# Cached index keys of a decode step: the query columns become the stationary operand in four column tiles, and the weighted sum over heads becomes two matrix products

## The chip, the cores and the metric

The kernel runs on one core of one Trainium2 chip. The metric is the device time of one execution in microseconds (us). All data are float32.

## The reference, cut to what matters

One layer is computed for 1024 prompt tokens and for 8 sample sequences of one new token each: a feed-forward half step, a mixer (sparse attention beside a gated recurrence), a second feed-forward half step. The change lies in the mixer, in the *indexer* of the sample sequences. Every sample sequence has 8192 cached index keys of 64 numbers, in 64 pages of 128 keys. Each key gets one score from eight index heads, and the 256 best keys are attended.

```python
def indexer_scores(qi, wi, kidx, valid):
    logits = jnp.einsum('bqhd,bld->bqhl', qi, kidx) * (HEAD_DIM_IDX ** -0.5)
    score = jnp.einsum('bqh,bqhl->bql', wi * (N_HEADS_IDX ** -0.5), jax.nn.relu(logits))
    return jnp.where(valid, score, -jnp.inf)
...
ki_past = cache_kidx[page_table].reshape(B, past, HEAD_DIM_IDX)
score = indexer_scores(qi, wi, ki_all, valid[None])
_, idx = lax.top_k(score, n_sel)
```

## The kernel before, in words

Five engines run programs of their own and meet at semaphores. The work follows an order written out by hand in each engine's program; nothing plans it at run time. TensorE computes the mixer's input projection in *units* (`unit`): one unit is 8 matrix products of 128 rows of contraction, each with 344 moving columns (L723) or 256 (L728). A float32 product leaves two records in the trace, so a unit leaves 16.

The part that the change touches is a loop of 32 rounds (`ROUNDS`), about 915 to 1125 us after the start of the span. In each round, one eighth of the pages of two sequences is scored, and beside it runs one step of a 32-step bitwise search for the threshold of the prompt's top 256 (`NBITS`). Round r on each engine:

- GpSimd gathers 128 rows of 1024 numbers (16 keys each) by an indirect DMA into one of four buffers `KX` (L614). Partitions 0 to 63 belong to one sequence, 64 to 127 to the other.
- TensorE turns the block by eight 128x128 transposes (L781, `turn_keys`), so that a pair of keys lies on the 128 partitions; it runs one unit; then `key_logits` (L790) makes eight products with 128 key columns stationary and 32 moving query columns `QB` (two parities of key, eight heads, two sequences). The result is 128 partitions by 256 numbers in PSUM bank 5 or 6.
- ScalarE copies the turned keys out of PSUM (`keys_out`, L1143), sums three compare results for the search (`pass_counts`, three L1149), and copies the unit's result (L1115).
- VectorE compares three score blocks for ScalarE (L1367) and counts three more itself (L1370). Then comes `reduce_keys` of the round before: two fused maximum-and-multiply operations on 64 partitions (L1322) and one reduction over the eight heads (L1326) into the score table `SDEC`. Then it waits for ScalarE's sums and does four small operations (L1376, L1353, L1354, L1355) that set the next candidate of the search.

Waits that couple the engines: transposes of round r wait until ScalarE has copied the keys of r-1; `key_logits` of r waits for the copied keys of r and for the reduction of r-2; ScalarE's sums come behind its copy of the keys, in its program order; the next search step on VectorE waits for ScalarE's sums.

Before the loop, GpSimd sends the sample queries through a scratch tensor to `QB` (L626, L630) and the head weights to `WDEC` (L633, L637), then issues output DMAs and four masks (L660). VectorE scales `WDEC` (L1346). After the loop TensorE waits for the last keys to be reduced and for VectorE's preparation of the recurrence (L1483 to L1490) before the level products (L856).

Of the kernel before, what the change touches and what calls it, by code (L numbers as in the profile page):

```python
# [9 lines left out]
def build_decoder_step(nc, I, O):  # L10
# [8 lines left out]
    ALU, ACT, AX = mybir.AluOpType, mybir.ActivationFunctionType, mybir.AxisListType  # L19

    P = 128
# [23 lines left out]
    with ctx:  # L45
# [319 lines left out]
        KXT = BIG[:, 3 * C4 + 2560:3 * C4 + 4608].rearrange("p (u c) -> p u c", c=1024)  # L365
        DPROD = BIG[:, 3 * C4 + 2048:3 * C4 + 2304].rearrange("p (u c) -> p u c", c=P)
        RELU = BIG[:, 3 * C4:3 * C4 + 2048].rearrange("p (u c) -> p u c", c=1024)
# [3 lines left out]
        def score(b):  # L371
# [8 lines left out]
        KIW = AUX[:, 0:9 * 72].rearrange("p (b c) -> p b c", c=72)  # L380
        WIS = AUX[:, 648:648 + 72].rearrange("p (b h) -> p b h", h=H)
        JUNK = BIG[:, o_kv + 2304:o_kv + 2560].bitcast(mybir.dt.uint8)
        DCMP = K3[:, 2, 9 * HD:9 * HD + 258].bitcast(mybir.dt.bfloat16).rearrange("p (g k) -> p g k", k=PAGE + 1)
# [35 lines left out]

        WDEC = SMALL[:, 0:32].rearrange("p (g h) -> p g h", h=H)  # L420
        DCNT, GTC, PCC = SMALL[:, 32:36], SMALL[:, 36:40], SMALL[:, 40:48]
# [13 lines left out]
        qi_s, q_s = dram("scratch_qi", [512, NB]), dram("scratch_q", [512, NB])  # L435
        w_s, sn_s = dram("scratch_w", [NB, H]), dram("scratch_new_score", [NB, 1])
        hid_s = dram("scratch_hidden", [P, FT * TOK]).rearrange("p (f t) -> p f t", t=TOK)
# [8 lines left out]
        qid_turned, sn_ready = sem("qid_turned"), sem("sn_ready")  # L446
        scratch_out, qb_zero, qb_in, w_in_dec, sn_in = (sem(x) for x in (
            "scratch_out", "qb_zeroed", "qb_in", "wdec_in", "sn_in"))
        sdec_filled = sem("sdec_filled")
# [156 lines left out]
        def pool_mixer(pool, G, link):  # L606
# [14 lines left out]
            G.memset(SDECF, NEG).then_inc(sdec_filled, 1)  # L621
            G.memset(QB[:, :, :, :], 0.0).then_inc(qb_zero, 1)
            nc_ok = nc.allow_non_contiguous_dma(reason="eight sample columns")
            with nc_ok:
                pool.wait_ge(unit_out, N1)
                pool.dma_start(qi_s.rearrange("(t p) b -> p t b", p=P), QIT[:, :, SEQ:TOK]).then_inc(scratch_out, 16)  # L626
                pool.wait_ge(scratch_out, 16)
                pool.wait_ge(qb_zero, 1)
                for par in range(2):
                    pool.dma_start(QB[64 * par:64 * par + 64, par, :, :],  # L630
                                   qi_s.rearrange("(h d) b -> d h b", d=HD)).then_inc(qb_in, 16)
                pool.wait_ge(wis_ready, 1)
                pool.dma_start(w_s, WIS[0:NB, 8, :]).then_inc(scratch_out, 16)  # L633
                pool.wait_ge(scratch_out, 32)
                for half in range(2):
                    src = w_s.rearrange("(g u) h -> u g h", u=2)[half:half + 1].to_broadcast([64, 4, H])
                    pool.dma_start(WDEC[64 * half:64 * half + 64, :, :], src).then_inc(w_in_dec, 16)  # L637

# [11 lines left out]
                pool.dma_start(sn_s, SN).then_inc(scratch_out, 16)  # L650
                pool.wait_ge(scratch_out, 48)
                pool.wait_ge(sdec_filled, 1)
# [50 lines left out]
        def pe_mixer(pe, cols, mean, var):  # L703
# [80 lines left out]
            def key_logits(r):  # L784
                gp = r // 8
                pe.wait_ge(kxt_a, r + 1)
                if r >= 2:
                    pe.wait_ge(dix_read, 2 * r - 2)
                for j in range(8):
                    last = M(PS[:, 5 + r % 2, 32 * j:32 * j + 32], KXT[:, r % 2, P * j:P * j + P],  # L790
                             QB[:, :, :, 2 * gp:2 * gp + 2], start=True, stop=True)
                last.then_inc(dix_done, 1)
            pe.wait_ge(qb_in, 32)
            for r in range(ROUNDS):
                turn_keys(r)
                unit(N1 + WOVEN + r)
                key_logits(r)
            pe.wait_ge(kxt_a, ROUNDS)
            pe.wait_ge(dix_read, 2 * ROUNDS)

# [283 lines left out]
        def act_mixer(act, A, link, square, sd, gain):  # L1084
# [54 lines left out]
            def keys_out(r):  # L1139
# [15 lines left out]

            def block_copy(t, lv):
# [116 lines left out]
        def dve_mixer(dve, V, link, step, centre, sqsum, scale):  # L1273
# [39 lines left out]

            def reduce_keys(r):
                gp, sub = divmod(r, 8)
                dve.wait_ge(dix_done, r + 1)
                if r >= 2:
                    dve.wait_ge(dix_red, r - 1)
                for half in range(2):
                    rows = slice(64 * half, 64 * half + 64)  # L1320
                    ps = PS[rows, 5 + r % 2, 0:256].rearrange("p (k h s) -> p k h s", h=H, s=2)[:, :, :, half]
                    V.scalar_tensor_tensor(DPROD[rows, r % 2, :].rearrange("p (k h) -> p k h", h=H), ps, 0.0,  # L1322
                                           WDEC[rows, gp:gp + 1, :].to_broadcast([64, 16, H]),
                                           ALU.max, ALU.mult).then_inc(dix_read, 1)
                dve.wait_ge(dix_read, 2 * r + 2)
                V.tensor_reduce(SDEC[:, gp, 16 * sub:16 * sub + 16],  # L1326
                                DPROD[:, r % 2, :].rearrange("p (k h) -> p k h", h=H), AX.X, ALU.add).then_inc(dix_red, 1)
            for i in range(6 * H):
# [33 lines left out]
            for i in range(NBITS):  # L1362
# [10 lines left out]
                if i:  # L1373
                    reduce_keys(i - 1)
# [3 lines left out]
            reduce_keys(NBITS - 1)  # L1378

            def sample_compare(k):  # L1380
                if k == 0:
                    dve.wait_ge(sn_in, 32)
                    dve.wait_ge(dix_red, ROUNDS)
# [1541 lines left out]
```

## Time and profile before

| | us |
|---|---|
| median of 3 runs | 2485.77 (2480.25 to 2489.41) |
| time of the profiled execution | 2480.91 |
| span of its trace | 2478.8 |
| TensorE matmul busy | 2392.3 (97%) |
| VectorE busy | 1684.4 (68%) |
| ScalarE busy | 698.6 (28%) |
| GpSimd busy | 861.4 (35%) |
| mean granted TensorE clock | 0.98 of full speed |

The 2.1 us between the span and the execution's time lie around the program. A busy share is an average over stages; the stage of the 32 rounds has to be read by itself. Matmul records overlap, so the pace of a run of matmuls is read from its starts, or from its piece in the chain of waits, not from the length of one record.

### The profile page before, as it was taken

How to read it: one execution, taken by the hardware profiler on the slowest of the kernel's cores; microseconds unless marked ns; L12 is line 12 of the kernel's file. 1: busy time of each engine (PE TensorE's matmuls, PEld its weight loads, DVE VectorE, ACT ScalarE, POOL GpSimd, SP SyncE). 2: the span in 40 equal slices, each digit the busy share in tenths (PEclk: the TensorE clock that was granted, in tenths of full speed). 3: DMA queues.
4: the chain of work that ended last, by engine and by line, in shares of the span. 5: the costliest groups of instructions: out<-in, count | busy, mean ns of one | idle time of the engine just before them, and what ended most of it. 6: DMA issues, size and time to landing. Idle time of an engine off the chain costs nothing.

```text
span 2478.8 us, 33700 instructions
## 1 busy us (share of the span) xinstructions
PE 2392.3 (97%) x12445; PEld 1986.0 (80%) x12445; DVE 1684.4 (68%) x2737; ACT 698.6 (28%) x1399; POOL 861.4 (35%) x916
## 2 busy tenths in 40 slices
PE   8999999999999999999998899999999999999996
PEld 7888888888886547887777777788888888888885
DVE  6666666588963287898777855435675665677886
ACT  2122222200033166662222245512322222210014
POOL 5344444445563111110000022413344444445570
PEclk9999999999999999999998889999999999999998
DMA  6021213374201213330000021112012222157301
GB/s 179 18 94 52 90 64 103 111 278 161 81 22 34 69 52 98 94 86 18 2 18 1 11 62 38 48 35 68 9 60 85 69 72 74 60 190 266 141 18 69
DMA packets 136928, 192.34 MB, mean 78 GB/s; under 512 B 18472, under 2 KB 85144, under 8 KB 136512
## 3 DMA queue, kind: packets, MB, share of 16 engines
q1 hardware_dynamic: 129328, 169.71, 20.5%
q0 software_dynamic: 7440, 20.49, 3.1%
q8 instruction: 102, 1.67, 0.3%
q14 instruction: 58, 0.48, 0.1%
HBM read 160.12 MB, written 30.06 MB: 77 GB/s over the span
## 4 chain that ended last, share of the span: by engine, by line
PE 86%; DVE 9%; issue 2%; ACT 2%; POOL 1%; DMA 1%; SPq 0%; DVEq 0%; POOLq 0%; ACTq 0%
PE ps L1955 37%; PE ps L2049 15%; PE ps L723 8%; PE ps L728 6%; PE ps L1068 4%; PE ps L956 2%; PE ps L790 2%; PE ps L930 2%; PE ps L2052 2%; PE ps L768 1%; PE ps L846 1%; PE ps L943 1%; PE ps L781 1%; ACT big L1135 1%; DVE big L1384 0%
## 5 line engine op out<-in xcount | busy, mean ns | idle before, releaser
L1955 PE MATMUL ps<-big 128*128 128x258 f32 x1760 | 410.5, 381 | 5.1 <-DVE big L2368 4.6
L1955 PEld LDWEIGHTS ps<-big 128*128 128x128 f32 x1760 | 333.0, 190 | 57.1 <-issue 7.7
L2220 ACT ACTIVATE down_weights<-ps 128x258 f32<-128x258 f32 x370 | 142.8, 387 | 700.4 <-PE ps L1955 700.3
L2488 DVE TENSOR_TENSOR down_weights<-ps,down_weights 128x258 f32<-128x258 f32 x330 | 139.4, 425 | 261.6 <-ACT down_weights L2220 186.9
L723 PE MATMUL ps<-acts,weight_ring 128*128 128x344 f32 x768 | 236.7, 458 | 0.0
L723 PEld LDWEIGHTS ps<-acts,weight_ring 128*128 128x128 f32 x768 | 141.8, 190 | 77.3 <-issue 12.4
L2049 PE MATMUL ps<-big,aux 128*128 128x258 f32 x840 | 193.1, 385 | 4.0 <-DVE big L2601 4.0
L2796 POOL TENSOR_TENSOR big<-weight_ring 128x256 f32<-128x256 f32 x100 | 75.3, 755 | 334.8 <-PE ps L1955 300.1
L2049 PEld LDWEIGHTS ps<-big,aux 128*128 128x128 f32 x840 | 160.8, 192 | 30.1 <-DVE big L2601 5.7
L728 PE MATMUL ps<-weight_ring,acts 128*128 128x256 f32 (+3 forms) x720 | 176.6, 401 | 0.0
L728 PEld LDWEIGHTS ps<-weight_ring,acts 128*128 128x128 f32 (+1 forms) x720 | 129.1, 184 | 34.1 <-issue 3.1
L2049 PE MATMUL ps<-big,weight_ring 128*128 128x258 f32 x600 | 137.5, 381 | 0.6 <-DVE weight_ring L2647 0.5
L1955 PE MATMUL ps<-big,aux 128*128 128x258 f32 x512 | 131.6, 381 | 0.9 <-DVE down_weights L2488 0.9
L2049 PEld LDWEIGHTS ps<-big,weight_ring 128*128 128x128 f32 x600 | 113.4, 190 | 19.2 <-issue 2.0
L1955 PE MATMUL ps<-big,weight_ring 128*128 128x258 f32 x480 | 120.8, 381 | 0.0
L1955 PE MATMUL ps<-acts,weight_ring 128*128 128x258 f32 x480 | 114.6, 382 | 4.0 <-DVE acts L1703 1.8
L1955 PE MATMUL ps<-weight_ring,big 128*128 128x258 f32 x464 | 118.1, 381 | 0.0
L1068 PE MATMUL ps<-big,weight_ring 128*128 128x258 f32 x512 | 113.4, 382 | 0.8 <-ACT big L1203 0.8
L1955 PEld LDWEIGHTS ps<-big,aux 128*128 128x128 f32 x512 | 96.9, 190 | 16.1 <-DVE down_weights L2488 1.7
L1068 PEld LDWEIGHTS ps<-big,weight_ring 128*128 128x128 f32 x512 | 96.9, 190 | 15.1 <-ACT big L1203 1.0
L1955 PEld LDWEIGHTS ps<-acts,weight_ring 128*128 128x128 f32 x480 | 90.7, 190 | 18.5 <-DVE acts L1703 2.2
L1955 PEld LDWEIGHTS ps<-big,weight_ring 128*128 128x128 f32 x480 | 91.1, 190 | 13.4
(443 smaller groups left out, 4605.8 us busy)
## 6 DMA issues: line engine op xcount, KB each, us to landing
big<-scratch_hidden SPq DMA_DIRECT2D x12, 2838.0 KB, 11.1
weight_ring<-ffn_wd SPq DMA_DIRECT2D x8, 2816.0 KB, 9.8
scratch_hidden<-down_weights SPq DMA_DIRECT2D x40, 516.0 KB, 2.8
weight_ring<-ffn_wg SPq DMA_DIRECT2D x20, 1024.0 KB, 7.9
weight_ring<-ffn_wu SPq DMA_DIRECT2D x20, 1024.0 KB
down_weights<-ffn_wd SPq DMA_DIRECT2D x4, 2816.0 KB, 20.7
weight_ring<-w_in SPq DMA_DIRECT2D x9, 1024.0 KB, 5.3
big<-x_prompt SPq DMA_DIRECT2D x8, 512.0 KB, 5.6
```

The source lines that it names most:

```text
L723: last = M(PS[:, unit_bank(u), 0:TW], w[:, k, P * a:P * a + P], ACTS[:, k, cols(x)], start=k == 0, stop=k == DT - 1)
L728: last = M(PS[0:rows, unit_bank(u), 0:a], ACTS[:, k, P * x:P * x + rows], w[:, k, :], start=k == 0, stop=k == DT - 1)
L790: last = M(PS[:, 5 + r % 2, 32 * j:32 * j + 32], KXT[:, r % 2, P * j:P * j + P], QB[:, :, :, 2 * gp:2 * gp + 2], start=True, stop=True)
L930: last = M(PS[:, k0, 0:min(512, n - c)], QT[rows, h // 2, P * b:P * b + P], K3[rows, h // 4, c:min(c + 512, n)], start=True, stop=True)
L956: last = M(PS[:, 2 + bi % 2, HD * h:HD * h + HD], probs_turned(i)[:, P * j:P * j + P], KV[:, j, c:c + HD], start=j == 0, stop=j == b)
L1068: last = M(PS[:, Y_BANK[y], 0:TQ], w[:, k, P * (d % 2):P * (d % 2) + P], src, start=k == 0, stop=k == DT - 1)
L1955: last = M(PS[:, 3 * e + bank, 0:TQ], lhs[:, i, :], rhs[:, i, :], start=begin and i == 0, stop=end and i == n - 1, skip_group_check=True)
L2049: last = M(PS[:, 3 * e + bank, 0:TQ], lhs[:, i, P * e:P * e + P], rhs[:, i, :], start=begin and i == 0, stop=end and i == 4 and rest is No ...
L2052: last = M(PS[:, 3 * e + bank, 0:TQ], rest[0][:, P * e:P * e + P], rest[1], start=False, stop=end, skip_group_check=True)
L2220: A(st(e, c), PS[:, 3 * e, 0:TQ], ACT.Copy).then_inc(cp_done, 1)
L2488: V.tensor_tensor(out, PS[:, 3 * e + bank, 0:TQ], st(e, part), ALU.add).then_inc(add_done, 1)
L2796: G.tensor_tensor(part(e, 2), operand(e, 0, 0), operand(e, 1, 0), ALU.subtract).then_inc(su_done, 1)
```

## The change

`key_logits` swaps its operands: the 32 query columns (rearranged by GpSimd into `QG`) are stationary, in four column tiles of 32 (PSUM partitions 0-31, 32-63, 64-95, 96-127), and each tile has 256 of the 1024 key columns moving. The head now lies on the partitions, so the weighted sum over heads is a contraction: VectorE only takes the maximum with zero (`relu_keys`, one operation on 128x256 from PSUM to `KREL`), and TensorE makes two products (`key_scores`) with 128 columns of `KREL` stationary and 16 columns of a small table `WSEL` moving, into PSUM bank 7. These come two rounds later, between the transposes and the unit. Every eight rounds ScalarE copies a finished table from bank 7 into `SDEC` (`page_scores`, two copies of 64x128). The table `WSEL` is built once by VectorE from the identity and the head weights, which GpSimd brings by two DMAs out and eight DMAs in.

```diff
@@ GpSimd, before the loop
-                pool.dma_start(w_s, WIS[0:NB, 8, :]).then_inc(scratch_out, 16)
-                pool.wait_ge(scratch_out, 32)
-                for half in range(2):
-                    src = w_s.rearrange("(g u) h -> u g h", u=2)[half:half + 1].to_broadcast([64, 4, H])
-                    pool.dma_start(WDEC[64 * half:64 * half + 64, :, :], src).then_inc(w_in_dec, 16)
+                for u in range(2):
+                    pool.dma_start(w_s[:, :, u], WIS[u:NB:2, 8, :]).then_inc(scratch_out, 16)
+                pool.wait_ge(scratch_out, 48)
+                pool.wait_ge(qb_in, 32)
+                G.tensor_copy(QG.rearrange("p g (x u) -> p g x u", u=2),
+                              QB.rearrange("p r h (g u) -> p g (r h) u", u=2)).then_inc(consts, 1)
+                for x in range(8):
+                    pool.dma_start(WROW[16 * x:16 * x + 16, :], w_s.rearrange("g h u -> (h u) g")).then_inc(w_in_dec, 16)
@@ TensorE
                 if r >= 2:
-                    pe.wait_ge(dix_read, 2 * r - 2)
-                for j in range(8):
-                    last = M(PS[:, 5 + r % 2, 32 * j:32 * j + 32], KXT[:, r % 2, P * j:P * j + P],
-                             QB[:, :, :, 2 * gp:2 * gp + 2], start=True, stop=True)
+                    pe.wait_ge(dix_read, r - 1)
+                for c in range(4):
+                    rows = slice(32 * c, 32 * c + 32)
+                    last = M(PS[rows, 5 + r % 2, 0:2 * P].rearrange("p (u x) -> p u x", u=2),
+                             QG[:, gp, :],
+                             KXT[:, r % 2, :].rearrange("p (u c x) -> p u c x", u=2, c=4)[:, :, c, :], start=True, stop=True)
                 last.then_inc(dix_done, 1)
+            def key_scores(r):
+                gp, sub = divmod(r, 8)
+                pe.wait_ge(dix_read, r + 1)
+                if gp and sub == 0:
+                    pe.wait_ge(dix_red, 2 * gp)
+                for j in range(2):
+                    at = 16 * sub + 8 * j
+                    last = M(PS[:, 7, 0:2 * P].rearrange("p (b c) -> p b c", b=2)[:, :, at:at + 8],
+                             KREL[:, r % 2, P * j:P * j + P], WSEL[:, gp, :, :], start=True, stop=True)
+                last.then_inc(dix_scored, 1)
             for r in range(ROUNDS):
                 turn_keys(r)
+                if r >= 2:
+                    key_scores(r - 2)
                 unit(N1 + WOVEN + r)
                 key_logits(r)
+            key_scores(ROUNDS - 2)
+            key_scores(ROUNDS - 1)
             pe.wait_ge(kxt_a, ROUNDS)
-            pe.wait_ge(dix_read, 2 * ROUNDS)
+            pe.wait_ge(dix_red, 8)
@@ ScalarE
+            def page_scores(gp):
+                act.wait_ge(dix_scored, 8 * gp + 8)
+                if gp == 0:
+                    act.wait_ge(sdec_filled, 1)
+                for half in range(2):
+                    rows = slice(64 * half, 64 * half + 64)
+                    A(SDEC[rows, gp, 0:PAGE], PS[rows, 7, P * half:P * half + PAGE], ACT.Copy).then_inc(dix_red, 1)
             for r in range(ROUNDS):
                 keys_out(r)
+                if r >= 9 and r % 8 == 1:
+                    page_scores(r // 8 - 1)
                 pass_counts(r)
                 unit(N1 + WOVEN + r)
+            page_scores(3)
@@ VectorE
-            def reduce_keys(r):
-                gp, sub = divmod(r, 8)
+            def relu_keys(r):
                 dve.wait_ge(dix_done, r + 1)
                 if r >= 2:
-                    dve.wait_ge(dix_red, r - 1)
-                for half in range(2):
...
-                    V.scalar_tensor_tensor(DPROD[rows, r % 2, :].rearrange("p (k h) -> p k h", h=H), ps, 0.0,
...
-                dve.wait_ge(dix_read, 2 * r + 2)
-                V.tensor_reduce(SDEC[:, gp, 16 * sub:16 * sub + 16],
...
+                    dve.wait_ge(dix_scored, r - 1)
+                V.tensor_scalar(KREL[:, r % 2, :], PS[:, 5 + r % 2, 0:2 * P], 0.0, None, ALU.max).then_inc(dix_read, 1)
-            dve.wait_ge(w_in_dec, 32)
-            dve.wait_ge(sdec_filled, 1)
-            link(V.tensor_scalar(WDEC, WDEC, KSCALE, None, ALU.mult))
+            dve.wait_ge(w_in_dec, 128)
+            link(V.tensor_reduce(PICK.rearrange("p (x b) -> p x b", b=2),
+                                 IDENT.rearrange("p (x h b) -> p x b h", h=H, b=2), AX.X, ALU.add))
+            for gp in range(4):
+                link(V.tensor_scalar(WSEL[:, gp, :, :].rearrange("p b x -> p x b"), PICK.rearrange("p (x b) -> p x b", b=2),
+                                     WROW[:, gp:gp + 1], KSCALE, ALU.mult, ALU.mult))
```

## Rows read from the trace of the kernel before

**Rows 1.** Page, part 1: busy us, share of the span, instructions.

```profile
PE 2392.3 (97%) x12445; PEld 1986.0 (80%) x12445; DVE 1684.4 (68%) x2737; ACT 698.6 (28%) x1399; POOL 861.4 (35%) x916
```

**Rows 2.** Chain that ended last, rounds 12 to 15 and its end: start us, us, what.

```profile
1000.70 4.63 PE ps L723 x16
1005.33 1.71 PE ps L790 x16
1007.03 0.91 PE ps L781 x8
1007.94 4.63 PE ps L723 x16
...
1021.25 3.46 PE ps L728 x16
1024.70 1.71 PE ps L790 x16
1026.40 0.91 PE ps L781 x8
1027.31 3.46 PE ps L728 x16
...
1100.18 1.78 DVE big L1367 x3
1106.02 1.88 DVE big L1367 x3
1111.95 1.88 DVE big L1367 x3
1117.89 2.65 DVE big L1367 x3
```

**Rows 3.** Timeline of one late round: start us, us, engine, line [idle before <-releaser].

```profile
1110.17 0.61 DVE L1322 SCALAR_TENSOR_TENSOR big<-ps,small 64x128 f32<-64x128 f32 x2
1110.82 0.28 DVE L1326 TENSOR_REDUCE down_weights<-big 128x16 f32<-128x128 f32 x1
1111.02 0.16 DVE L1376 TENSOR_SCALAR rejected<-counts 128x6 int32<-128x6 f32 x1
```

**Rows 4.** Timeline of an earlier round, transposes to the next search step.

```profile
1081.13 1.07 PE L781 MATMUL ps<-ident,weight_ring 128*128 128x128 f32 x8
1082.24 1.02 ACT L1143 ACTIVATE big<-ps 128x1024 f32<-128x1024 f32 x1 [1.98 <-PE ps L781]
1085.96 0.37 ACT L1115 ACTIVATE big<-ps 128x256 f32<-128x256 f32 x1
1086.08 0.17 DVE L1376 TENSOR_SCALAR rejected<-counts 128x6 int32<-128x6 f32 x1
1087.02 1.88 DVE L1367 TENSOR_SCALAR big<-down_weights,candidate 128x1024 f32<-128x1024 f32 x3
```

**Rows 5.** Timeline of products on parts of the array: row halves (L768), column halves (L901).

```profile
908.72 1.99 PE L768 MATMUL ps<-big 64*128 64x512 f32 x8 [0.33 <-ACT big L1135]
910.63 0.85 PE L723 MATMUL ps<-acts,weight_ring 128*128 128x344 f32 x2
1200.13 1.15 PE L901 MATMUL ps<-big 128*64 128x64 f32 x32
```

**Rows 6.** Chain that ended last, the same products: whole array (L896), column halves (L901).

```profile
1196.44 3.75 PE ps L896 x32
1200.20 1.11 PE ps L901 x32
```

**Rows 7.** Groups of VectorE, by form: plain copies out of PSUM, mean ns of one.

```profile
L2329 DVE COPY acts<-ps 128x512 f32<-128x512 f32 x10 | 6.4, 686 | 8.0 <-PE ps L1930 8.0
L1286 DVE COPY big<-ps 128x384 f32<-128x384 f32 x8 | 4.4, 553 | 41.4 <-PE ps L739 41.4
```

**Rows 8.** Timeline of GpSimd and VectorE before the loop.

```profile
862.62 1.28 POOL L637 DMA_DIRECT2D small<-scratch_w  x2 [3.94 <-DMA scratch_w<-aux]
...
914.52 0.18 DVE L1346 TENSOR_SCALAR small<-small 128x32 f32<-128x32 f32 x1
914.92 0.29 POOL L660 TENSOR_SCALAR_AFFINE_SELECT down_weights<-down_weights 128x128 f32<-128x128 f32 x1 [12.66 <-DVE down_weights L1340]
915.31 2.09 DVE L1367 TENSOR_SCALAR big<-down_weights,candidate 128x1024 f32<-128x1024 f32 x3 [0.61 <-POOL down_weights L660]
```

**Rows 9.** Timeline of round 28's extra VectorE step and behind the loop.

```profile
1099.16 0.82 DVE L1359 TENSOR_SCALAR big<-big,lower_bound 128x1032 f32<-128x1032 f32 x1
...
1124.59 0.61 DVE L1322 SCALAR_TENSOR_TENSOR big<-ps,small 64x128 f32<-64x128 f32 x2
1125.48 0.11 DVE L1558 MEMSET big<- 128x64 f32 x1
1127.47 3.79 PE L856 MATMUL ps<-big 64*128 64x128 f32 x32 [3.42 <-DVE down_weights L1490]
```

More of the change, by code:

```diff
@@ L365, in build_decoder_step @@
         KXT = BIG[:, 3 * C4 + 2560:3 * C4 + 4608].rearrange("p (u c) -> p u c", c=1024)
-        DPROD = BIG[:, 3 * C4 + 2048:3 * C4 + 2304].rearrange("p (u c) -> p u c", c=P)
+        KREL = BIG[:, 3 * C4 + 1024:3 * C4 + 1536].rearrange("p (u c) -> p u c", c=2 * P)
         RELU = BIG[:, 3 * C4:3 * C4 + 2048].rearrange("p (u c) -> p u c", c=1024)
@@ L381, in build_decoder_step @@
         WIS = AUX[:, 648:648 + 72].rearrange("p (b h) -> p b h", h=H)
+        WSEL = AUX[:, 720:784].rearrange("p (g b x) -> p g b x", g=4, b=2)
+        PICK, WROW = AUX[:, 784:800], AUX[:, 800:804]
+        QG = AUX[:, 804:932].rearrange("p (g x) -> p g x", g=4)
         JUNK = BIG[:, o_kv + 2304:o_kv + 2560].bitcast(mybir.dt.uint8)
@@ L418, in build_decoder_step @@
         NORMG = sb("norm_g", [P, 4])
-        WDEC = SMALL[:, 0:32].rearrange("p (g h) -> p g h", h=H)
         DCNT, GTC, PCC = SMALL[:, 32:36], SMALL[:, 36:40], SMALL[:, 40:48]
@@ L435, in build_decoder_step @@
         qi_s, q_s = dram("scratch_qi", [512, NB]), dram("scratch_q", [512, NB])
-        w_s, sn_s = dram("scratch_w", [NB, H]), dram("scratch_new_score", [NB, 1])
+        w_s, sn_s = dram("scratch_w", [NB // 2, H, 2]), dram("scratch_new_score", [NB, 1])
         hid_s = dram("scratch_hidden", [P, FT * TOK]).rearrange("p (f t) -> p f t", t=TOK)
@@ L446, in build_decoder_step @@
         qid_turned, sn_ready = sem("qid_turned"), sem("sn_ready")
-        scratch_out, qb_zero, qb_in, w_in_dec, sn_in = (sem(x) for x in (
-            "scratch_out", "qb_zeroed", "qb_in", "wdec_in", "sn_in"))
+        scratch_out, dix_scored, qb_in, w_in_dec, sn_in = (sem(x) for x in (
+            "scratch_out", "dix_scored", "qb_in", "wdec_in", "sn_in"))
         sdec_filled = sem("sdec_filled")
@@ L621, in pool_mixer @@
             G.memset(SDECF, NEG).then_inc(sdec_filled, 1)
-            G.memset(QB[:, :, :, :], 0.0).then_inc(qb_zero, 1)
+            link(G.memset(QB[:, :, :, :], 0.0))
             nc_ok = nc.allow_non_contiguous_dma(reason="eight sample columns")
@@ L627, in pool_mixer @@
                 pool.wait_ge(scratch_out, 16)
-                pool.wait_ge(qb_zero, 1)
                 for par in range(2):
@@ L650, in pool_mixer @@
                 pool.dma_start(sn_s, SN).then_inc(scratch_out, 16)
-                pool.wait_ge(scratch_out, 48)
+                pool.wait_ge(scratch_out, 64)
                 pool.wait_ge(sdec_filled, 1)
@@ L787, in key_logits @@
                 if r >= 2:
-                    pe.wait_ge(dix_read, 2 * r - 2)
-                for j in range(8):
-                    last = M(PS[:, 5 + r % 2, 32 * j:32 * j + 32], KXT[:, r % 2, P * j:P * j + P],
-                             QB[:, :, :, 2 * gp:2 * gp + 2], start=True, stop=True)
-                last.then_inc(dix_done, 1)
-            pe.wait_ge(qb_in, 32)
+                    pe.wait_ge(dix_read, r - 1)
[4 more added lines that the diff above has]
+                             KXT[:, r % 2, :].rearrange("p (u c x) -> p u c x", u=2, c=4)[:, :, c, :], start=True, stop=True)
+                last.then_inc(dix_done, 1)
+            def key_scores(r):
[8 more added lines that the diff above has]
+                last.then_inc(dix_scored, 1)
+            pe.wait_ge(consts, 4)
             for r in range(ROUNDS):
                 turn_keys(r)
+                if r >= 2:
+                    key_scores(r - 2)
                 unit(N1 + WOVEN + r)
                 key_logits(r)
+            key_scores(ROUNDS - 2)
+            key_scores(ROUNDS - 1)
             pe.wait_ge(kxt_a, ROUNDS)
-            pe.wait_ge(dix_read, 2 * ROUNDS)
+            pe.wait_ge(dix_red, 8)
             def count(k):
@@ L1312, in dve_mixer @@
             dve.wait_ge(wis_ready, 1)
-            def reduce_keys(r):
-                gp, sub = divmod(r, 8)
+            def relu_keys(r):
                 dve.wait_ge(dix_done, r + 1)
                 if r >= 2:
-                    dve.wait_ge(dix_red, r - 1)
-                for half in range(2):
-                    rows = slice(64 * half, 64 * half + 64)
-                    ps = PS[rows, 5 + r % 2, 0:256].rearrange("p (k h s) -> p k h s", h=H, s=2)[:, :, :, half]
-                    V.scalar_tensor_tensor(DPROD[rows, r % 2, :].rearrange("p (k h) -> p k h", h=H), ps, 0.0,
-                                           WDEC[rows, gp:gp + 1, :].to_broadcast([64, 16, H]),
-                                           ALU.max, ALU.mult).then_inc(dix_read, 1)
-                dve.wait_ge(dix_read, 2 * r + 2)
-                V.tensor_reduce(SDEC[:, gp, 16 * sub:16 * sub + 16],
-                                DPROD[:, r % 2, :].rearrange("p (k h) -> p k h", h=H), AX.X, ALU.add).then_inc(dix_red, 1)
+                    dve.wait_ge(dix_scored, r - 1)
+                V.tensor_scalar(KREL[:, r % 2, :], PS[:, 5 + r % 2, 0:2 * P], 0.0, None, ALU.max).then_inc(dix_read, 1)
             for i in range(6 * H):
@@ L1373, in dve_mixer @@
                 if i:
-                    reduce_keys(i - 1)
+                    relu_keys(i - 1)
                 dve.wait_ge(summed, 3 * i + 3)
@@ L1377, in dve_mixer @@
                 next_bit(slice(0, 6), i)
-            reduce_keys(NBITS - 1)
+            relu_keys(NBITS - 1)
             def sample_compare(k):
@@ L1382, in sample_compare @@
                     dve.wait_ge(sn_in, 32)
-                    dve.wait_ge(dix_red, ROUNDS)
+                    dve.wait_ge(dix_red, 8)
                 link(V.tensor_tensor(DCMP, SDEC, cand[:, 6:10].unsqueeze(2).to_broadcast([P, 4, PAGE + 1]), ALU.is_ge))
```

## The prediction

> **What bounds the kernel now.** First the page: TensorE is busy 97% of the span, VectorE 68% [rows 1]. That says that TensorE time is worth most in general, and nothing yet of the changed loop. So next the chain of waits over the loop's stretch. In the rounds whose unit has 344 columns a round is three TensorE pieces without a gap: transposes 0.91, unit 4.63, key logits (L790) 1.71 us, 7.24 us from one start to the next (1000.70 to 1007.94). In the rounds with 256 columns it is 0.91 + 3.46 + 1.71 = 6.07 (1021.25 to 1027.31) [rows 2]. I count 14 rounds of the first kind (8 query units, 6 gate units) and 18 of the second. From about 1100 us on the chain is no longer TensorE's: it names VectorE, and the search steps start at 1106.02, 1111.95, 1117.89, that is 5.93 us apart [rows 2]. So VectorE without idle time needs 5.93 us a round, only 0.14 less than TensorE in the second kind. That is the first thing to keep in mind: in 18 of 32 rounds a faster TensorE alone would gain almost nothing; what the change does on VectorE counts as much.
>
> **TensorE, the logits.** Removed: 16 records in 1.71 us, 0.107 each, though only 32 columns move: the pace is that of loading 128 stationary columns. Added: four products of 256 moving columns, 8 records. The unit's pace gives 4.63 / 16 / 344 = 0.84 ns per column and record, so 0.215 us for one record of 256 columns. One behind the other, eight take 1.72 us; four side by side, two steps of 0.215 = 0.43.
> Four tiles side by side are not in the trace; two are. Column halves (L901): 32 records of 64 columns, 0.054 us each by the same pace, would take 1.72 us in a row; they took 1.11 including the last one's way out, and the whole-array products of the same width (L896) 3.75 [rows 6]. Row halves (L768): 8 records of 512 columns, 0.43 each, would take 3.44 in a row; the unit's next record starts 1.91 us after their first [rows 5]. So two tiles run fully at once, and entering and leaving the tiled layout costs 1.91 - 4 x 0.43 = 0.19. The ends for the new logits: 0.43 + 0.19 = 0.62 us (four at once), 8 x 0.215 + 0.19 = 1.91 (one by one). I take 0.62, since both kinds of halves reached their full overlap and neither shows a loss that would grow with a third and fourth; it is nearest to them.
> The Trainium skill speaks against this: TensorE: Matmul & The Clock Gate, Part 3, says that a weight load overlaps running matmuls only when the row group differs, and column tiles share it. If so L901 would have paid 64 columns of load for every record, besides the matmul. The trace disagrees: 32 records in 1.11 us. By the page's figure for three column tiles, 2.38 times, my estimate is 1.72 / 2.38 = 0.72 for the logits before the cost of switching, near the low end.
>
> **TensorE, the sums.** Added per round from the third on: two products with 128 stationary and 16 moving columns, 4 records. They are of L790's kind, bound by the load: 4 x 0.107 = 0.43 us. The lower end is a hidden load, nearly 0; the upper is the mean of an unhidden record, about 0.27, so 1.1. I take 0.43, because L790's records with 32 moving columns ran at this pace [rows 2].
> TensorE per round: 7.24 - 1.71 + 0.62 + 0.43 = 6.58, and 6.07 - 1.09 + 0.43 = 5.41. The first two rounds have no sums: 6.15.
>
> **VectorE.** Removed per round: the two L1322 and L1326, from 1110.17 to the start of L1376 at 1111.02, 0.85 us [rows 3]. Added: one maximum on 128x256 out of PSUM. Plain copies out of PSUM take 553 ns for 384 columns and 686 for 512 [rows 7], 1.04 ns a column, so 0.42 us for 256. The next instruction started before the end of L1326 (0.20 after a start with 0.28 of length), so I count 0.36; the ends are 0.27 (halved rate) and 0.46. VectorE's own round becomes 5.93 - 0.85 + 0.36 = 5.44 us. It is equal to TensorE's 5.41 in the second stage, so that I take 5.45 there.
>
> **Waits.** TensorE now waits for the maximum of round r-2 before the unit, not before the logits of r; behind it stand the unit and the logits. That maximum belongs to search step r-1, whose end lies at or before the start of round r's transposes as now; the sums stand 0.9 us later, and even if TensorE runs up to 1 us ahead they are not late. The loop through ScalarE: from a round's transposes to the next search step it is 5.89 us (1081.13 to 1087.02) [rows 4]: copy of the keys, three sums, four small operations. This spans two rounds' starts and is not a cycle by itself, since the copy waits only for the transposes; ScalarE's own work is 1082.24 to 1086.33, 4.1 us of 5.45. ScalarE's two page copies every eighth round, each at most the 0.37 of a 128x256 copy [rows 4], stand ahead of the sums on which the search waits: about 0.6 us in rounds 17 and 25, together 1.2 at most, 0.9 taken. Those in round 9 fall into TensorE's slack.
>
> **Before and behind the loop.** GpSimd gets one more DMA out and six more in, at 0.64 us each [rows 8] 4.5 us, a copy and a wait for the queries: about 5 us. Queued behind are six output DMAs, the new score and the masks L660; the last of these had waited 12.66 us for VectorE, so it hides this, and the keys' gather behind it starts as before. VectorE builds the table in five small operations instead of one, about 1 us; 0.61 of it lies in the wait for L660 [rows 8], the rest in VectorE's slack of the first stage. If that cover were gone, it would cost 0.4 once. Behind the loop the final reduction (1124.59 to 1125.48, 0.89 us) becomes one maximum, 0.44: 0.45 gained. TensorE's last sums and ScalarE's last page copies (0.4 + 0.6 and two handovers) run beside VectorE's preparation, which takes from 1125.48 to 1127.47 [rows 9]; I cost them at nothing, 0.5 at worst. The rest of the kernel moves up as a block.
>
> **The sum.** First stage: 2 x (7.24 - 6.15) + 12 x (7.24 - 6.58) = 10.1 us. Second stage: the step after round 14 starts 5.89 after its transposes, at 1019.9 now and at 1009.9 then; the loop's last step ends at 1124.59 [rows 9], 104.7 later. Then: 17 x 5.45 = 92.7, plus 0.93 for the extra forget-gate step L1359 of round 28 [rows 9], which VectorE no longer hides, plus 0.9 for the page copies: 94.5. Gain 10.2. With 0.45 behind: 20.7 us. The profiled execution took 2480.91 us (2.1 beside its span), so 2460.2; the median is 4.9 higher, so I forecast 2465 us for the median.
>
> **Rivals.**
> A, two at a time. The array runs only two column tiles at once, which is all that the rows show. The logits take 4 x 0.215 + 0.19 = 1.05; rounds are 7.01 and 5.84, and TensorE bounds both stages. First stage 2 x 0.66 + 12 x 0.23 = 4.1; second 104.7 - 17 x 5.84 - 0.5 = 4.9; with the end 9.5 gained: 2476.
> B, in order. Each product's second record holds up the next product, so that only neighbours overlap: five steps of 0.215, 1.27 with the switch. Rounds are 7.23 and 6.06; gain 1 in the first stage, about 1.5 in the second: 2483, no change. The page's rule that matmuls start and end in program order would do this here. Against it: L768's 8 records need 5 steps by this, 2.15 us, before the unit may start; it started after 1.91 [rows 5].
> C, slower. Four separate key streams out of the same partitions are served one by one: logits 1.91, place TensorE's round, price 0.20 in the first two rounds and 0.63 in the 30 others, 19.3 us, less about 2 which VectorE's excess at the end of the loop now costs: 2485.8 + 17 = 2503. It turns to slower when the logits take over 1.28 us. For it: no row has more than two streams. Against it: two streams cost each other nothing measurable.
> D, the new wait on the maximum or ScalarE's copies stop TensorE by about 0.5 us in each late round: 20.7 - 18 x 0.5, 12 gained: 2474.
>
> **How the numbers follow.** Forecast 0.55 (its own range 2457 to 2472), A 0.13, B 0.07, C 0.13, D 0.12. What can be told from no change is 0.5%, 12.4 us, so under 2473.4 is faster. Faster: 0.55, half of D: 0.61. Same: A, B, the other half of D, 0.26. Slower: C, 0.13. The range 2456 to 2487 leaves out C and little below.
>
> **What would show it.** In the changed kernel's chain the L781 pieces should stand 6.58 and then 5.45 us apart, the logits 0.62 before the next transposes, their records starting in fours; the four records of the sums 0.43 us; the maximum 0.42 us; in the late rounds no VectorE idle time of note. Starts of the logits' records in pairs mean A, at 0.215 distance C. The forecast is wrong if rounds of the second kind take over 5.8 us, or if the stages behind the loop don't move up as a block, TensorE's clock among them: L856's 32 records take 3.79 us after an idle of 3.42 [rows 9], 0.12 each, and where the granted clock falls anew or doesn't fall, 3 us move either way.

## The result

The changed kernel takes 2457.77 us (median of 4 runs, 2454.58 to 2459.49), the kernel before, beside it, 2484.09 (4 runs, 2480.25 to 2489.41). The ratio is 0.9895, 95% interval 0.9881 to 0.9910: 26.3 us less. The forecast was 2465 in a range of 2456 to 2487, so the time lies inside, but near its low end; 20.7 us of gain were forecast. The runs of one kernel differ by 5 to 9 us, and the profiled one is at the fast end for both; the two spans differ by 26.0 us, as the medians do.

Both profiles side by side, from marks that mean the same in both (us in the trace):

| | before | after | gained |
|---|---|---|---|
| first transposes of the loop | 912.73 | 912.67 | 0.1 |
| transposes of round 14 (first round of 256 columns) | 1014.1 | 1005.2 | 8.9 |
| last maximum or reduction begins | 1124.59 | 1106.18 | 18.4 |
| first level products | 1127.47 | 1108.57 | 18.9 |
| end of the span | 2478.8 | 2452.8 | 26.0 |

So 18.9 us come from the changed loop and 7.1 from the stretch behind it, where not one instruction differs.

The page, part 1 (answers to [rows 1]):

```profile
PE 2365.9 (96%) x12317; PEld 1940.7 (79%) x12317; DVE 1669.7 (68%) x2677; ACT 701.8 (29%) x1407; POOL 865.2 (35%) x924
```

The chain that ended last, rounds of both kinds (start us, us, what). L785 are the transposes, L795 the logits, L807 the sums, L727 and L732 the unit (answers to [rows 2]):

```profile
998.56 1.03 PE ps L785 x8
999.58 0.35 PE ps L807 x4
999.94 4.72 PE ps L727 x16
1004.66 0.57 PE ps L795 x8
1005.23 1.02 PE ps L785 x8
1006.60 3.55 PE ps L732 x16
1010.15 0.57 PE ps L795 x8
1010.72 1.03 PE ps L785 x8
```

The reader is to see 6.67 us from 998.56 to 1005.23, where 7.24 were before, and 5.49 from 1005.23 to 1010.72, where 6.07 were. The logits' piece is 0.57 instead of 1.71.

VectorE's side in a late round, from the timeline (answers to [rows 3]). The maximum L1351 takes 0.42 us and L1403 starts 0.34 after it; search steps start 5.43 us apart (L1394):

```profile
1089.21 1.88 DVE L1394 TENSOR_SCALAR big<-down_weights,candidate 128x1024 f32<-128x1024 f32 x3
1093.37 0.42 DVE L1351 TENSOR_SCALAR big<-ps 128x256 f32<-128x256 f32 x1
1093.71 0.16 DVE L1403 TENSOR_SCALAR rejected<-counts 128x6 int32<-128x6 f32 x1
1094.64 1.88 DVE L1394 TENSOR_SCALAR big<-down_weights,candidate 128x1024 f32<-128x1024 f32 x3
```

The end of the loop (answers to [rows 9]): TensorE's last sums wait for the last maximum, ScalarE's last page copies follow, and the level products L877 still wait for VectorE alone:

```profile
1106.66 0.62 PE L807 MATMUL ps<-aux,big 128*128 128x16 f32 x4 [0.65 <-DVE big L1351]
1107.32 0.57 ACT L1173 ACTIVATE down_weights<-ps 64x128 f32<-64x128 f32 x2 [2.60 <-PE ps L807]
1108.57 3.27 PE L877 MATMUL ps<-big 64*128 64x128 f32 x32 [1.29 <-DVE down_weights L1517]
```

### The profile page after: what moved, and what is told of

It reads as the page before. It is cut to its first block, busy times and chain, and to the rows that moved or that the text cites. A ratio compares the mean times of both kernels' runs of the same rounds, so it can differ in the third digit from the quotient of the medians.

```text
span 2452.8 us, 33405 instructions
## 1 busy us (share of the span) xinstructions
PE 2365.9 (96%) x12317; PEld 1940.7 (79%) x12317; DVE 1669.7 (68%) x2677; ACT 701.8 (29%) x1407; POOL 865.2 (35%) x924
## 3 DMA queue, kind: packets, MB, share of 16 engines
q1 hardware_dynamic: 129328, 169.71, 20.7%
## 4 chain that ended last, share of the span: by engine, by line
PE 86%; DVE 9%; issue 2%; ACT 1%; POOL 1%; DMA 1%; SPq 0%; DVEq 0%; POOLq 0%; ACTq 0%
PE ps L1982 38%; PE ps L2076 15%; PE ps L727 8%; PE ps L732 6%; PE ps L1089 4%; PE ps L977 2%; PE ps L2079 2%; PE ps L951 1%; PE ps L772 1%; PE ps L785 1%; PE ps L867 1%; PE ps L964 1%; PE ps L795 1%; ACT big L1156 1%; DVE big L1411 0%
## 5 line engine op out<-in xcount | busy, mean ns | idle before, releaser
L727 PE MATMUL ps<-acts,weight_ring 128*128 128x344 f32 x768 | 237.5, 459 | 0.0
L727 PEld LDWEIGHTS ps<-acts,weight_ring 128*128 128x128 f32 x768 | 141.8, 190 | 77.2 <-issue 12.2
L732 PE MATMUL ps<-weight_ring,acts 128*128 128x256 f32 (+3 forms) x720 | 177.7, 402 | 0.0
L732 PEld LDWEIGHTS ps<-weight_ring,acts 128*128 128x128 f32 (+1 forms) x720 | 129.1, 184 | 33.8 <-issue 2.8
```

What stands on the lines that cost most here:

```text
L727: last = M(PS[:, unit_bank(u), 0:TW], w[:, k, P * a:P * a + P], ACTS[:, k, cols(x)], start=k == 0, stop=k == DT - 1)
L732: last = M(PS[0:rows, unit_bank(u), 0:a], ACTS[:, k, P * x:P * x + rows], w[:, k, :], start=k == 0, stop=k == DT - 1)
```

## Experiments

"Loop" is the time from the first transposes to the first level products, "behind" from there to the end of the span, both from the one profile of each kernel; "time" is the median of runs, with its ratio to the kernel before on the same chip. Five more kernels or repeats with one run each stand under "The time behind the loop".

| kernel | loop | behind | time | ratio (95%) |
|---|---|---|---|---|
| before | 214.7 | 1351.3 | 2484.09 | |
| after | 195.9 | 1344.2 | 2457.77 | 0.9895 (0.9881 to 0.9910) |
| one tile | 234.5 | 1342.7 | 2494.68 | 1.0049 (1.0030 to 1.0069) |
| two tiles | 207.3 | 1342.7 | 2469.01 | 0.9939 (0.9918 to 0.9959) |
| no score products | 190.1 | 1352.4 | 2458.55 | 0.9898 (0.9871 to 0.9925) |
| VectorE's work back | 203.4 | 1352.0 | 2469.02 | 0.9927 (0.9908 to 0.9945) |
| before, less VectorE work | 214.0 | 1352.1 | 2482.57 | 0.9991 (0.9979 to 1.0002) |
| logits in pairs | 197.6 | 1345.5 | 2460.38 | 0.9902 (0.9875 to 0.9930) |
| pairs, early maximum | 192.8 | 1347.0 | 2455.75 | 0.9887 (0.9871 to 0.9904) |

### Do the four tiles run at once, and does it matter?

```diff
@@ key_logits, all in one tile
-                    rows = slice(32 * c, 32 * c + 32)
+                    rows = slice(0, 32)
@@ key_logits, two tiles by turns
-                    rows = slice(32 * c, 32 * c + 32)
+                    rows = slice(32 * (c % 2), 32 * (c % 2) + 32)
```

> The four products of the logits all go to the first column tile (PSUM partitions 0 to 31), so they can't run side by side; three quarters of the sample keys' scores are not computed rightly by this. Theory (the gain on TensorE is that four tiles run at once): 8 records of 0.215 one behind the other instead of two steps, 1.29 us more a round, rounds 7.96 and 6.79; 32 x 1.29 = 41 us less about 1.5 that VectorE bounds now: 2497 us, slower than the kernel before. Rival (the gain is the 32-column stationary load that replaces the 128-column one, and the overlap is not needed): rounds stay within 0.2 of 6.67 and 5.50, 2458 to 2464 us.

> The four products of the logits go to two column tiles by turns (partitions 0 to 31, 32 to 63), so that at most two can run side by side; half of the sample keys' scores are not computed rightly. Theory (each tile works through its own queue, and all tiles run at once): four steps of 0.215 instead of two, 0.43 us more a round, rounds 7.10 and 5.93, in all 13.8 us more than the change less 1 at the end: 2470 us. Rival (a product's second record holds up the next product, so that neighbours overlap only by halves): five steps, 0.65 us more a round, 2477 us. Rival (what matters is only whether the tiled layout is used): as the changed kernel, 2458 us.

Measured: 2494.68 us, slower than before, and 2469.01. First the timeline of the changed kernel in a stretch that ends at 1065.12, 0.2 us after the logits began; the count on the second line is what to read:

```profile
1064.60 0.38 PE L732 MATMUL ps<-weight_ring,acts 128*128 128x256 f32 x1
1064.91 0.42 PE L795 MATMUL ps<-big,aux 128*32 128x256 f32 x4
```

Four records are under way at once. With all products in one tile the records start 0.21 us apart, so these four belong to four tiles, and none of them waited behind the second record of another. The eight weight loads stand within 0.16 us beside them:

```profile
1064.91 0.16 PEld L795 LDWEIGHTS ps<-big,aux 128*32 128x32 f32 x8 [0.33 <-issue]
```

The chain of the kernel with one tile, and then of that with two:

```profile
1085.40 1.02 PE ps L785 x8
1086.43 0.35 PE ps L807 x4
1086.78 3.55 PE ps L732 x16
1090.33 1.84 PE ps L795 x8
```

```profile
1036.29 1.02 PE ps L785 x8
1037.31 0.35 PE ps L807 x4
1037.66 3.55 PE ps L732 x16
1041.21 0.99 PE ps L795 x8
1042.20 1.02 PE ps L785 x8
```

The pieces of the logits are 0.57, 0.99 and 1.84 us for four, two and one tile: 0.42 us for two steps more and 1.27 for six, 0.21 us a step, as 256 columns should take. The rounds are 7.94 and 6.77 us with one tile, 7.09 and 5.91 with two. Nothing is lost between two and four streams out of the same partitions. The loop of one tile, 234.5 us, is 19.8 us longer than before the change: this is rival C of the prediction, made by hand; it had priced itself at 17. The rival that the narrow weight load is the gain by itself falls.

### Which engine sets the second stage?

```diff
@@ relu_keys: VectorE's work back
+                link(V.tensor_scalar(BIG[:, 3 * C4 + 2048:3 * C4 + 2304], PS[:, 5 + r % 2, 0:2 * P], 0.0, None, ALU.max))
                 V.tensor_scalar(KREL[:, r % 2, :], PS[:, 5 + r % 2, 0:2 * P], 0.0, None, ALU.max).then_inc(dix_read, 1)
@@ key_scores: no score products but in each eighth round
-                for j in range(2):
+                for j in range(2 if sub == 7 else 0):
...
@@ reduce_keys of the kernel before: less VectorE work
-                for half in range(2):
+                for half in range(1):
...
-                V.tensor_reduce(SDEC[:, gp, 16 * sub:16 * sub + 16], ...).then_inc(dix_red, 1)
+                V.memset(SDEC[:, gp, 16 * sub:16 * sub + 16], 0.0).then_inc(dix_red, 1)
```

> The maximum is taken twice, once into an unused place, so that VectorE has about the work of before again (5.43 + 0.46 = 5.89 us a round) while TensorE has the new products. Theory (VectorE's relief carries the gain in the second stage): late rounds 5.89 us apart instead of 5.50, the first stage unchanged at 6.67; 6.6 us and 0.5 at the end lost: 2465 us. Rival (TensorE's products alone carry the gain): 2458 us, rounds 5.50.

> The two products of the weighted sum are left out in seven of eight rounds (the sample scores are then not computed); maximum and page copies stay. Theory (two limits close together: TensorE 6.67 and 5.50, VectorE 5.43): the first stage gains 0.45 a round, 12 x 0.45 x 7/8 = 4.7 us; the second stage only 5.50 to 5.43, about 1.2 us: 6 us in all, 2452 us. Rival (TensorE alone bounds the loop): 0.45 in all 30 rounds, 12 to 13 us, 2445 us.

> The kernel before with about VectorE's new load and TensorE's old one: one of the two L1322 and the reduction L1326 are left out (half of the products and the sums of the sample scores are then missing), VectorE 5.93 to 5.4 us a round. Theory (TensorE bounds all but the last rounds of the kernel before): rounds stay 7.24 and 6.07 apart; only the end, where VectorE was the later, gains about 1.5 us and 0.4 behind the loop: 2482 us. Rival (VectorE's relief is worth by itself what putting its work back costs): 6 to 7 us, 2478 us.

(Not shown of the second edit: the semaphore of the sums rises by 8 with the last of eight, and the maximum waits for that.)

VectorE's work back: the search steps of the second stage start 5.89 us apart and the loop is 7.5 us longer than after the change (7.1 expected). Its chain names VectorE, and TensorE's sums wait for the maxima:

```profile
1079.80 0.44 DVE big L1351
1080.26 0.43 DVE big L1352
1080.69 0.04 issue
1080.74 0.62 PE ps L807 x4
1081.35 3.55 PE ps L732 x16
1084.90 0.61 PE ps L795 x8
```

No score products: rounds of 6.22 us in the first stage, and in the second VectorE's chain without a TensorE piece, 5.43 us from one L1395 to the next:

```profile
1040.91 1.88 DVE big L1395 x3
1042.79 0.81 DVE big L1398 x2
...
1046.34 1.88 DVE big L1395 x3
```

The loop gains 5.8 us (6 expected). The time doesn't: 2458.55, because "behind" is 8.2 us longer; that is taken up below.

The kernel before with less VectorE work needs 5.48 us for a search step where nothing else holds it, and keeps its TensorE rounds, 6.07 us:

```profile
1027.81 0.91 PE ps L781 x8
1028.71 3.46 PE ps L728 x16
1032.17 1.71 PE ps L790 x16
1033.88 0.91 PE ps L781 x8
```

Its loop gains 0.8 us, against about 1.9 expected. So of the 18.9 us in the loop TensorE's part alone gives 11.4 (214.7 to 203.4), VectorE's part alone about 0.8, and 6.7 come only when both are there. Both kernels copy the other state to within 0.05 us a round (VectorE 5.89 for 5.93, and 5.48 for 5.43).

### The time behind the loop

> The kernel before once more, for a second profile. In the first pair of profiles the change gained 18.9 us up to the level products behind the loop, and the span 26.0 us: 7 us more behind the loop, where no instruction differs. Theory: these 7 us are TensorE's granted clock, whose half-speed spells behind 1100 us fell otherwise in the two profiles (in the profile of before 20.5 us at half speed from 1429 us on, in that of after 10.2 us). It expects the spells of this second profile of before to differ from the first's in place or length, and the stretch from the first level products to the end to vary by some us. Rival: the spells belong to the kernel and the earlier arrival at a stage shortens a real wait there; it expects this profile to repeat the first's stretch within 1 us.

> The changed kernel once more, for a second profile. Both theories expect the loop as in the first: rounds 6.67 and 5.50 us apart. Clock theory: the stretch from the first level products to the end may come out some us longer or shorter than the first's 1344 us. Rival (a real wait is shorter): the same within 1 us.

```diff
@@ the loop on TensorE (n = 2 and 4 in the changed kernel, 3 in the kernel before)
+                if r == 2:
+                    pad(N1 + WOVEN + r, n)   # n products of 344 columns into the unit's bank, before the unit
                 unit(N1 + WOVEN + r)
```

> The changed kernel with two more products of 344 columns in round 2 (their result is overwritten), 1.16 us of TensorE time; nothing else differs. The question is the stretch from the first level products behind the loop to the end: 1351.3 us in the kernel before, 1344.2 in the changed one, and both repeat in a second profile. Theory (the half-speed spells of the granted clock hang on the time at which the stretch begins, not on what the change does in it): the stretch differs from 1344.2 by over 1 us here or in one of the other two shifted kernels. Rival (the earlier arrival shortens a wait, or the clock hangs only on the work before): 1344.2 within 0.5, and the whole kernel 1.2 us longer.

> The changed kernel with four more products of 344 columns in round 2, 2.31 us. Theory (the clock's spells hang on when the stretch behind the loop begins): the stretch from the first level products to the end differs from 1344.2 us by over 1 us here or in the other shifted kernels. Rival: 1344.2 within 0.5, the whole 2.3 us longer.

> The kernel before with three more products of 344 columns in round 2, 1.74 us. Theory (clock by the time of arrival): its stretch of 1351.3 us behind the loop changes by over 1 us, and could fall to that of the changed kernel, so that the kernel gets faster by added work. Rival (a property of the kernel's work): 1351.3 within 0.5, the whole 1.7 us longer.

| kernel | level products begin | behind | TensorE at half speed |
|---|---|---|---|
| before | 1127.47 | 1351.3 | 84 |
| before again | 1129.07 | 1351.0 | 83 |
| before, 1.7 us added | 1130.37 | 1352.6 | 86 |
| before, less VectorE work | 1128.10 | 1352.1 | 87 |
| after | 1108.57 | 1344.2 | 64 |
| after again | 1110.50 | 1344.2 | 64 |
| after, 1.2 us added | 1109.67 | 1346.9 | 74 |
| after, 2.3 us added | 1111.71 | 1344.9 | 67 |
| one tile, two tiles | 1148.69, 1121.55 | 1342.7, 1342.7 | 60, 60 |
| logits in pairs; with early maximum | 1112.30; 1107.76 | 1345.5; 1347.0 | 64; 74 |
| no score products; VectorE's work back | 1104.67; 1115.38 | 1352.4; 1352.0 | 80; 80 |

The last column is the length of the 1.2 GHz spells in the trace's record of the granted clock, from 10 us ahead of the level products to the end of the span. The same instructions take 1342.7 to 1352.6 us. The six profiles with 60 to 67 us at half speed have 1342.7 to 1345.5, the two with 74 have 1346.9 and 1347.0, the six with 80 to 87 have 1351.0 to 1352.6. Second profiles repeat the first to 0.4 us, so the clock theory's expectation of run-to-run changes fell.

Work added in round 2 lengthened the stretch by 2.6 us (1.2 us added) and 0.7 (2.3 added) in the changed kernel and by 1.2 (1.7 added) in the kernel before. Two of these are over 1 us, as the theory of arrival expected, and its rival, no effect over 0.5 us, falls. But the time of arrival is not what decides: both second profiles reached the level products later as well, by 1.6 and 1.9 us, because the loop began later, and their stretches stayed. Nor does the change grow with the work added.

Where a difference of this kind lies is seen in tables by stretches from the level products on (columns: stretch, its length, busy us of PE, PEld, DVE, ACT, POOL, then the granted clock as a share of 2.4 GHz). First the kernel before with 1.7 us added, then the changed kernel with 1.2 us added:

```profile
1230.37:1410.37 180.00, 168.41 (x1261) 135.85 (x1259) 143.06 (x239) 42.62 (x64) 4.10 (x4) 0.91 0.03 7
1410.37:1530.37 120.00, 107.82 (x744) 84.07 (x744) 75.14 (x165) 59.67 (x96) 24.47 (x24) 0.86 0.18 48
```

```profile
1209.67:1389.67 180.00, 168.44 (x1261) 135.94 (x1260) 143.07 (x239) 42.62 (x64) 4.11 (x4) 0.91 0.03 7
1389.67:1509.67 120.00, 106.61 (x785) 83.81 (x784) 80.26 (x171) 62.43 (x100) 25.52 (x25) 0.91 0.18 47
```

Up to 280 us behind the level products, the first 100 us included, the busy times of the two agree within 0.1 us; in the next 120 us, where the prompt's attention begins, the clock is 0.86 in one and 0.91 in the other. In their clock records a spell at half speed begins at the same place in both, 304 us behind the level products, and lasts 20.5 us in the one and 10.2 in the other.

For the 7.1 us between the kernel before and the changed kernel the starts can be compared one by one: VectorE has the same 1405 records behind the level products in both. Two of them, first in the kernel before, then in the changed kernel, stand 11.84 us apart in the one and 7.02 in the other:

```profile
1438.31 1.02 DVE L1467 SCALAR_TENSOR_TENSOR weight_ring<-down_weights,candidate,weight_ring 128x768 f32<-128x768 f32 x1
1450.15 0.96 DVE L1615 CUSTOM_DVE_ANT_0 weight_ring<-ps,down_weights 128x768 f32<-128x768 f32 x1 [4.81 <-PE ps L930]
```

```profile
1418.45 1.02 DVE L1494 SCALAR_TENSOR_TENSOR weight_ring<-down_weights,candidate,weight_ring 128x768 f32<-128x768 f32 x1
1425.47 0.96 DVE L1642 CUSTOM_DVE_ANT_0 weight_ring<-ps,down_weights 128x768 f32<-128x768 f32 x1 [2.17 <-PE ps L951]
```

The clock of 9 us in between, again before and after (last three columns: clock, DMA share, GB/s), is 0.50 in the one and 1.00 in the other, with 40 and 72 matrix products:

```profile
1440.00:1449.00 9.00, 9.00 (x40) 7.34 (x38) 1.67 (x4) 3.25 (x6) 1.20 (x2) 0.50 0.06 15
1421.10:1430.10 9.00, 9.00 (x72) 7.36 (x72) 3.14 (x8) 6.38 (x12) 2.04 (x3) 1.00 0.06 16
```

That is 4.8 of the 7.1 us. Of the rest, 0.7 lies in the level products themselves, which run at half speed for longer in the kernel before (4.9 us against 3.4); 1.0 comes in small steps where the clocks differ, up to 380 us behind them; 0.4 comes between 380 and 600 us, where both are at full speed, and is of the size by which two profiles of one kernel differ; 1.7 are lost again where the changed kernel alone has a spell, at 700 us, and 1.7 won where the kernel before alone has one, at 1305 us.

What that shows: the 7.1 us are, but for some tenths, granted clock, not a wait that the change removed. What it leaves open: why the spells fall as they do. The kernels with the old loop (4 profiles) and the two with the change but VectorE as the bound (no score products, VectorE's work back) have the long stretch, the other eight profiles the short one. What bounds the loop does not sort them: the kernel with early maximum, whose second stage is VectorE's too, is among the eight. In the shifted pair shown above the starts agree within 0.2 us up to 311 us behind the level products. Shifts of 1 to 2 us did not carry either kernel over to the other group.

### Entering the tiled layout half as often

```diff
-                if r >= 2:
-                    key_scores(r - 2)
+                if r >= 3:
+                    key_scores(r - 3)
                 unit(N1 + WOVEN + r)
-                key_logits(r)
+                if r % 2:
+                    key_logits(r - 1)
+                    key_logits(r)
@@ VectorE: in the first version behind the three counts, in the second ahead of them
-                if i:
-                    relu_keys(i - 1)
+                if i > 1:
+                    relu_keys(i - 2)
...
```

> The logits of two rounds are made back to back in the second of them, so that TensorE enters and leaves the tiled layout once in two rounds; the maximum and the sums come one round later. Theory (entering and leaving costs 0.19 to 0.23 us a time beyond the steps): TensorE saves 0.115 a round, first stage 6.67 to 6.55, second from 5.50 to VectorE's 5.43; 1.6 + 1.2 us less 0.4 for the second maximum behind the loop: 2.4 us, 2455 us. Rival (the excess is the first weight load and the drain of each run of logits, whatever stands beside it, so a run of 16 records saves nothing more than one start): the same saving would then show half, 6.61; or a new wait on the maximum (two of them now come late) costs more than it saves: 2460 us.

> The logits in pairs as in the run before it, where the second of a pair had waited for the maximum of the round before; here the maximum stands ahead of VectorE's three counts in each search step, some 2.3 us earlier. The first pair of that run, which had nothing to wait for, took 12.16 us for two rounds against 12.44 unpaired: 0.14 us a round for one entry into the tiled layout less. Theory (the wait on the maximum ate the saving): pairs of rounds 13.06 us in the first stage (6.53 a round) and twice VectorE's 5.43 in the second; from the first transposes to the level products 195.9 - 1.9 - 1.2 + 0.4 = 193.2 us, 2455 us if the clock behind the loop is as in the changed kernel. Rival (the uneven rounds, 4.8 and 6.0 us, break the step that VectorE and ScalarE share, wherever the maximum stands): over 195.9 us, no gain.

(Not shown of the edit: the third sum and the second maximum behind the loop, and ScalarE's page copies, one round later.)

The first version lost 1.7 us in the loop. Its timeline shows the wait that its expectation named as a rival: the second logits of the pair stand until the maximum L1353 is through, and TensorE idles:

```profile
1026.44 0.42 DVE L1353 TENSOR_SCALAR big<-ps 128x256 f32<-128x256 f32 x1
1027.02 0.64 PE L795 MATMUL ps<-big,aux 128*32 128x256 f32 x8 [0.51 <-DVE big L1353]
```

With the maximum ahead of the counts all 16 records run through in 1.07 us, against 2 x 0.64 for two single runs:

```profile
1025.36 1.07 PE L795 MATMUL ps<-big,aux 128*32 128x256 f32 x16
1026.36 1.09 PE L785 MATMUL ps<-ident,weight_ring 128*128 128x128 f32 x8
```

Its loop is 192.8 us, 3.1 less than after the change (193.2 were expected), and the second stage is VectorE's, with search steps of 5.43 to 5.58. Behind the loop it took 2.8 us more, with 10 us more at half speed, so that the time, 2455.75 us, 0.9887 (0.9871 to 0.9904) of before, can't be told from that of the changed kernel. It is the better loop; whether it is the faster kernel isn't settled.

## Why the prediction was right, and where it was not

- **What bounds.** Right. Two limits close together: TensorE's rounds are 5.50 us, with three exceptions of up to 0.14, to the end of the loop, and from round 17 VectorE runs beside it without a pause. The search step of round 17, with ScalarE's page copies, is 6.09 us, and the seven behind it are 5.43. The last steps, which end the loop, are VectorE's.
- **Logits: four at once.** Right in the mechanism, short in the size. The term was 0.62 with the change of layout. The first two rounds have no sums and take 6.22 us, forecast 6.15, so the term is 0.69: a logits' piece of 0.57, and 0.12 in the transposes behind it, whose piece is 1.03 and was 0.91:

```profile
918.96 1.03 PE ps L785 x8
919.99 4.63 PE ps L727 x16
924.62 0.57 PE ps L795 x8
```

- **Rivals.** A, B and C all fall on the timeline's four records at once. A and C were made by hand as well: their loops are 11.4 and 38.6 us longer than the changed one, expected 12.8 and 39.5.
- **The rule on weight loads.** The Trainium skill, TensorE: Matmul & The Clock Gate, Part 3, has weight loads of one row group not overlap running matmuls. The eight narrow loads here fall into 0.16 us, beside running matmuls; the trace does not agree. The strict program order that the same section has for starts and ends would make five steps if the two records of a product stand side by side in the stream, as rival B took them to; the trace has two. Which record belongs to which product it doesn't tell.
- **Sums.** Taken 0.43, measured 0.45 (6.67 with, 6.22 without). The rounds are 6.67 and 5.50 for 6.58 and 5.41 (5.45 with VectorE): 0.07 of the 0.09 is the logits' term, 0.02 the sums'. Over the first stage this is 1.2 us of gain not got (8.9 for 10.1), over the second 0.7 (9.5 for 10.2).
- **VectorE.** Right: 5.44 forecast, 5.43 measured; the maximum 0.42.
- **Waits.** Right: inside the loop the sums found the maximum ready in all rounds but one, which lost 0.12 us. The wait is real once VectorE is later, as with its work back. Page copies: the search step is 0.66 us longer than 5.43 in round 17 and 0.39 in round 25, together 1.05 for 0.9 taken.
- **Covers.** Right in effect. GpSimd came to its masks 5.8 us later (880.50 for 874.70), but an earlier wait than the one that the prediction named took it up: the third mask had waited 4.93 us and waits no more, the last still waits 12.35 us of 12.66. VectorE's first search step began 0.59 us later (915.90 for 915.31), which the slack of the first stage took up: TensorE's first rounds kept their 6.22.
- **Behind the loop.** The step that failed is "the rest of the kernel moves up as a block". The median gained 26.3 us for 20.7. The loop gave 18.9 for 20.7; the stretch behind it gave 7.1 for nothing. The prediction named the clock as what could spoil this and gave it 3 us; it moved 7. With the stretch of the kernel without score products behind it, the same loop would have gained some 18 us in all. The loop alone would give 2484.09 - 18.9 = 2465.2 us, the forecast's 2465; but that is luck too: the 1.8 us that the loop fell short are made up by the median of the kernel before, which is 2485.77 in the forecast and 2484.09 in the result.

## What to carry to other kernels

Small stationary operands belong in column tiles: four products of 32 columns ran in the time of one, at a fixed price of 0.26 us for each time the layout is entered and left (0.69 less two steps of 0.215), so they should stand together. Where two engines have nearly the same round, relieving one is worth little and relieving both is worth more than the sum: from round 14 on TensorE's part alone gave 2.7 us here, VectorE's 0.8, both together 10.0. Look for the second engine's round before pricing the first. A gain of a few us measured on a whole kernel whose TensorE waits often may be the clock: compare marks in the profiles, not ends.

## What was not expected of the hardware

- The same instructions behind the loop took 1342.7 to 1352.6 us in 14 profiles of 12 kernels, with 60 to 87 us at half clock, and a second profile of the same kernel repeats its value within 0.4 us. Leaving out 5.8 us of work in the loop gained nothing in time for this reason.
- Four moving streams out of the same 128 partitions, 256 float32 columns each, cost each other nothing: 0.21 us a step with one, two or four tiles.
